# A hybrid decoder step, attention stage: VectorE's sample steps in other places, the last values loaded ahead of the gate tensor, GpSimd's products between the last six units

## The reference, cut to what matters

```python
p_c = _masked_probs(s_c, mask_c)
o_c = jnp.einsum('bqgrn,bngd->bqgrd', p_c.astype(v_cmp.dtype), v_cmp)
...
p_s = _masked_probs(s_s, mask_s[:, :, :, None, :])
o_s = jnp.einsum('bqgrk,bgqkd->bqgrd', p_s.astype(vg.dtype), vg)
...
p_w = _masked_probs(s_w, mask_w)
o_w = jnp.einsum('bqgrk,bkgd->bqgrd', p_w.astype(v_win.dtype), v_win)
return gates[..., 0:1] * o_c + gates[..., 1:2] * o_s + gates[..., 2:3] * o_w
...
br_b = jnp.einsum('btc,cd->btd', jax.nn.silu(zb) * yb, w_out_b)
```

## Time and profile before

| what | value |
|---|---|
| time, median of 3 runs | 2439.54 us (2439.12 to 2439.92) |
| profiled execution | 2440.18 us, of which span 2438.4 us |
| TensorE matmul busy | 2358.7 us (97%) |
| VectorE busy | 1228.0 us (50%) |
| ScalarE busy | 987.5 us (40%) |
| GpSimd busy | 208.4 us (9%) |
| mean granted TensorE clock | 0.993 |
| attention stage, units | about 810 to 1054 us in layer 0, 2019 to 2261 us in layer 1 |

### The profile page before, as it was taken

The page is one execution under the profiler, slowest core; times in us unless marked ns, Lnnn a source line. Parts: engine busy times, 40 slices in busy tenths (PEclk is TensorE's granted clock), DMA queues, the critical chain, the costliest instruction groups (busy, mean ns, idle before and its releaser), DMA issues.

```text
span 2438.4 us, 45717 instructions
## 1 busy us (share of the span) xinstructions
PE 2358.7 (97%) x18047; PEld 2065.0 (85%) x18047; DVE 1228.0 (50%) x2324; ACT 987.5 (40%) x2024; POOL 208.4 (9%) x349
## 2 busy tenths in 40 slices
PE   8999999999999999899989999999999999998998
PEld 8999999997788655589989999999977885555998
DVE  4444232546675566564454432224567656665544
ACT  4232223435564455532333221234446545554332
POOL 0000000000000233310000000000000002334000
PEclk9999999999999999999999999999999999999999
DMA  6343354707642677663234334547086318867530
GB/s 236 121 138 104 87 169 124 162 19 159 90 50 35 107 121 121 124 197 112 85 127 137 123 104 96 169 115 162 5 172 88 52 19 135 120 111 163 165 115 37
DMA packets 293309, 279.10 MB, mean 114 GB/s; under 512 B 92601, under 2 KB 281465, under 8 KB 291816
## 3 DMA queue, kind: packets, MB, share of 16 engines
q1 hardware_dynamic: 288680, 239.34, 44.9%
q0 software_dynamic: 4416, 36.85, 4.1%
HBM read 249.25 MB, written 43.53 MB: 120 GB/s over the span
## 4 chain that ended last, share of the span: by engine, by line
PE 88%; DVE 5%; ACT 3%; DMA 1%; issue 1%; SPq 1%; DVEq 0%; POOL 0%; ACTq 0%
PE ps L771 47%; PE ps L1016 13%; PE ps L942 7%; PE ps L1143 3%; PE ps L1167 3%; PE ps L1126 2%; PE ps L969 2%; DVE chL L2127 2%; PE ps L1265 2%; PE ps L1041 1%; ACT chH L1646 1%; DMA v_win<-in_state_win 1%; PE ps L1413 1%; SPq L569 1%; PE ps L1273 1%
## 5 line engine op out<-in xcount | busy, mean ns | idle before, releaser
L771 PE MATMUL ps<-hH,wH 128*128 128x272 f32 x2016 | 418.7, 289 | 8.4 <-DVE hL L1970 8.3
L771 PE MATMUL ps<-hH,wL 128*128 128x272 f32 x2016 | 420.4, 290 | 0.0
L405 DVE TENSOR_TENSOR wL<-w_raw,wH 128x2048 fp32r<-128x2048 f32 (+1 forms) x107 | 246.1, 2300 | 346.2 <-ACT wH L396 343.9
L771 PE MATMUL ps<-hL,wH 128*128 128x272 f32 x2016 | 417.4, 289 | 0.0
L771 PEld LDWEIGHTS ps<-hH,wH 128*128 128x128 f32 x2016 | 318.7, 189 | 10.2 <-issue 7.5
L771 PEld LDWEIGHTS ps<-hH,wL 128*128 128x128 f32 x2016 | 317.4, 189 | 0.0
L771 PEld LDWEIGHTS ps<-hL,wH 128*128 128x128 f32 x2016 | 317.4, 189 | 0.0
L2127 DVE TENSOR_TENSOR chL<-ps,chH 64x256 fp32r<-64x256 f32 x512 | 216.5, 423 | 158.9 <-ACT chH L1646 151.3
L1646 ACT ACTIVATE chH<-ps 64x256 fp32r<-64x256 f32 x512 | 206.8, 404 | 214.5 <-PE ps L1016 205.9
L396 ACT ACTIVATE wH<-w_raw 128x2048 fp32r<-128x2048 f32 (+1 forms) x107 | 204.8, 1914 | 97.3 <-PE ps L771 77.6
L741 POOL TENSOR_SCALAR pr<-pr,inv,zg 128x512 f32<-128x512 f32 (+3 forms) x256 | 153.0, 607 | 966.1 <-DVE inv L2317 966.1
(11 more groups left out here) (337 smaller groups left out, 4037.9 us busy)
## 6 DMA issues: line engine op xcount, KB each, us to landing
w_raw<-in_w_in SPq DMA_DIRECT2D x59, 1024.0 KB
craw<-in_cache_kv SPq DMA_DIRECT2D x256, 128.0 KB, 5.1
w_raw<-in_w_in SPq DMA_DIRECT2D x64, 256.0 KB
k_sel<-in_cache_kv SPq DMA_DIRECT2D x128, 128.0 KB, 5.5
v_sel<-in_cache_kv SPq DMA_DIRECT2D x128, 128.0 KB, 10.5
out_new_win_sample<-in_state_win POOLq DMA_DIRECT2D x16, 1016.0 KB, 6.1
w_raw<-in_w_out_a SPq DMA_DIRECT2D x8, 1024.0 KB
k_win<-in_state_win SPq DMA_DIRECT2D x16, 512.0 KB, 6.9
```

The costliest lines, as they stand in the source:

```text
L405: dve.tensor_tensor(block_part(wL, b), block_part(w_raw, b), block_part(wH, b).bitcast(F32), ALU.subtract).then_inc(w_lo, 1)
L771: last = nc.tensor.matmul(ps[:, bank + hf, 0:HALF], st, x[:, k, hf * HALF:(hf + 1) * HALF], start=k == 0 and w is wH and x is xH, stop=k = ...
```

## The change

Three engines' orders change; no operation is added or taken away.

SyncE: the load of `zbs` stands behind the values of pair 3, where it stood ahead of them. GpSimd: the seven products of `zbs` stood ahead of the scaling of unit 58; now two stand behind it and one behind each of units 59 to 63. VectorE: the gains of the back pair are computed behind the maxima at k = 2 (was k = 3), the first multiplication into `sy` joins the other two behind the maxima at k = 4 (was k = 3), and at k = 6 the inverses and the turned copy of the next and this unit are done ahead of `copy_turned` (were behind it, at k = 7).

```diff
--- before.py
+++ after.py
@@ -632,10 +632,10 @@
                         sp.wait_ge(s_fin, 4 * l + pair - 1)
                         load_half(l, pair - 1, numbers, 3, v_sel, v_win, s_v)
                     numbers, ahead = ahead, page_numbers(pair + 1) if pair < 3 else None
+                sp.wait_ge(s_fin, 4 * l + 3)
+                load_half(l, 3, numbers, 3, v_sel, v_win, s_v)
                 sp.wait_ge(sa_kt, 48 * l + 48)
                 sp.dma_start(zbs[:], a["zb_keep"][l].rearrange("k p t -> p k t")).then_inc(zb_back, 16)
-                sp.wait_ge(s_fin, 4 * l + 3)
-                load_half(l, 3, numbers, 3, v_sel, v_win, s_v)
 
                 def load_ob(i):
 
@@ -729,11 +729,6 @@
 
                 for i in range(UNITS):
                     n, at_u = P * (unit(i)[2] + 1), UNITS * l + i
-                    if i == 58:
-                        pool.wait_ge(zb_back, 16 * l + 16)
-                        pool.wait_ge(pa_o, 8 * l + 7)
-                        for c in range(KT - 1):
-                            pool.tensor_tensor(zbs[:, c, 0:SEQ], zbs[:, c, 0:SEQ], yT[:, c, 0:SEQ], ALU.mult).then_inc(a_p, 1)
                     gp, r, u, br = unit(i)
                     pool.wait_ge(pa_inv, at_u + 1)
                     for g in range(2):
@@ -741,6 +736,11 @@
                         last = pool.tensor_scalar(pr[i % 3][:, g, 0:n], pr[i % 3][:, g, 0:n], inv[:, i % 3, g:g + 1], zg[:, u, gate:gate + 1],
                                                   ALU.mult, ALU.mult)
                     last.then_inc(pa_sc, 1)
+                    if i == 58:
+                        pool.wait_ge(zb_back, 16 * l + 16)
+                        pool.wait_ge(pa_o, 8 * l + 7)
+                    for c in {58: (0, 1), 59: (2,), 60: (3,), 61: (4,), 62: (5,), 63: (6,)}.get(i, ()):
+                        pool.tensor_tensor(zbs[:, c, 0:SEQ], zbs[:, c, 0:SEQ], yT[:, c, 0:SEQ], ALU.mult).then_inc(a_p, 1)
 
                 pool.wait_ge(m_f, 8 * l + 8)
                 pool.dma_start(pin[:, 0:NT, :], a["p_prompt"][ds(l, 1)].rearrange("l b (t p) d -> p (l b t) d", p=P)).then_inc(p_in, 16)
@@ -2380,7 +2380,7 @@
                     last.then_inc(sa_drop, 1)
                     dve.drain()
 
-                def combine_first(pair, bank):
+                def combine_gains(pair):
 
                     c = 92 + 2 * (pair % 2)
                     dve.wait_ge(s_fin, 4 * l + pair + 1)
@@ -2389,12 +2389,12 @@
                     dve.reciprocal(small[:, 77:79], small[:, 96:98])
                     dve.drain()
                     dve.tensor_tensor(small[:, 80:83], grow[:, pair, :], small[:, 76:79], ALU.mult)
+
+                def combine(pair, bank):
+
+                    dve.wait_ge(sa_yt, 4 * l + pair)
                     dve.drain()
-                    dve.wait_ge(sa_yt, 4 * l + pair)
                     dve.tensor_scalar(sy[:], ps[:, bank, 0:P], small[:, 80:81], None, ALU.mult)
-
-                def combine_rest(bank):
-
                     for n in (1, 2):
                         dve.drain()
                         last = dve.scalar_tensor_tensor(out=sy[:], in0=ps[:, bank, n * P:(n + 1) * P], scalar=small[:, 80 + n:81 + n], in1=sy[:],
@@ -2466,7 +2466,7 @@
                 for i in range(UNITS):
                     mm, k = divmod(i, 8)
                     back, front = sample_block(mm)
-                    if i:
+                    if i and (k < 7 or back is None):
                         inverses(i)
                         turned(i - 1)
                     if k == 1 and (back, front) != (None, None):
@@ -2475,10 +2475,10 @@
                         maxima(i + 2)
                     if k == 3 and front is not None:
                         sample_bias(front, 1, swsc)
-                    if k == 3 and back is not None:
-                        combine_first(back, 6 + (mm + 1) % 2)
+                    if k == 2 and back is not None:
+                        combine_gains(back)
                     if k == 4 and back is not None:
-                        combine_rest(6 + (mm + 1) % 2)
+                        combine(back, 6 + (mm + 1) % 2)
                     if i == 1:
                         sample_gates()
                     elif i == 3:
@@ -2486,6 +2486,8 @@
                     elif i == 5:
                         sample_probs()
                     if k == 6 and back is not None:
+                        inverses(i + 1)
+                        turned(i)
                         copy_turned(mm)
                     if i == 62:
                         dve.wait_ge(zb_back, 16 * l + 16)
```

## The result

The changed kernel takes **2451.75 us** (median of 4 runs, 2449.72 to 2454.08) where the kernel before took 2439.33 us beside it (2436.01 to 2439.92): 12.4 us slower, a ratio of 1.0054 with a 95% interval of 1.0037 to 1.0071. The direction is the forecast one, the size is not: 2446.0 us were forecast, with a range up to 2451.0. The profiled execution took 2449.72 us, its span of 2447.9 us is 9.5 us longer than before, and all that follows accounts for these 9.5.

The account below looks back on a forecast made before the run. TensorE was taken as busy almost throughout, gains possible only where it waits. Per layer 0.6 + 2.5 + 0.5 - 0.4 = 3.2 us, twice 6.4, took 2439.54 to 2446.0 us; range 2440.5 to 2451.

Parts of the forecast that it names:

- What bounds the stage: Attention stage's end: the 4.6 us values wait goes; the weight block then holds `output(57)`, with TensorE idle some 6 us.
- Rival 1: Weight block not held, landing well earlier: `output(57)` 6.2 us sooner, 3.7 us per layer gained, 2432 us; chance 0.15.
- Part 1: Values loaded ahead of `zbs`: values land near 1022.1, weight block shifts +0.6 us per layer, bounds 0 and 1.1.
- Part 2: GpSimd's seven products among units 58 to 63 delay `output(63)`: +2.5 us per layer, bounds 0 and 8.6.
- GpSimd busy without a gap: Expected profile sign: GpSimd has no idle gap from unit 58 to the seventh product; gaps there would refute the prediction.
- Part 3: TensorE's half clock moves onto units 57 to 60, mostly hidden: +0.5 us per layer, bounds 0 and 1.0.
- keeps its distance: What follows `output(63)` (`put_out`, the split of `zbs`, the first tile) was to follow it at the same distance as before.
- Part 4: VectorE's moves in blocks 2, 4, 6, 7: 0.2 us each in blocks 2 and 4, -0.4 us per layer.
- nothing more: Behind unit 6 of a block, inverses ahead of `copy_turned` leave VectorE's total up to the next maxima unchanged: no further gain.
- The rule that was set aside: VectorE two-SBUF-input operations and GpSimd SBUF reads exclude each other; only the sample-column product would meet it, changing neither sum nor chances.
- the forecast's 0.54: Chance given to the forecast case, 2442.5 to 2451 us; the part above 2444.4 was to count as slower.

Follow-up runs that it names:

- weights first: Changed kernel with the first block of `w_out_b` issued between the last values and the gate tensor `zbs`: 2440.65 us.
- copy first: Changed kernel with `a_high(0)` and `a_low(0)` placed behind the turned copy of unit 63: 2446.30 us.
- gate in two: Changed kernel, unit 63 turned before `a_high(0)`, `a_low(0)`; `zbs` chunks 0-2 before values, 3-7 after weight block; products 0-2 before scaling 58, one behind each of 59-62: 2433.67 us.

## Why the prediction was right about the side and wrong about the size

**What bounds the stage: right.** The wait of L1235 for a transfer is gone in both layers, the values landed near 1021, 8.5 us behind their last issue at 1012.45 (forecast 1022.1), the weight block decides, TensorE idles 6.7 us ahead of `output(57)` (some 6 forecast), and `output(57)` stands at T + 6.15 (6.2). Rival 1, that the weights are not held, did not come about; the kernel with the weights first, where the block is early, gains 11 us, of the 14 that rival 1 and the forecast lie apart.

**Part 1 (the weight block's shift, +0.6 us per layer): not told from the forecast.** In the pair of profiled executions T - v0 grew by 0.1 and 2.2 us. Over the traces with the old order (three kernels, six values) it is 30.9 to 35.5, mean 32.9; with the new one (six kernels, twelve values) 33.4 to 34.9, mean 34.3. That is +1.4, above my upper bound of 1.1, but the six values of the old order scatter so much that the difference is uncertain by more than 1 us either way (an estimate from their spread). Why the old order scatters by more than 4 us and the new one by 1.5 is open.

**Part 2 (GpSimd's products, +2.5 us per layer): the chain was right, its end was not.** Step by step behind T, forecast and measured in layer 0: scaling 59 at 9.3 and 9.63, scaling 63 at 18.68 to 19.56 and 19.24, end of the seventh product at 20.80 and 21.62, ScalarE's copy at 21.45 and 22.21, `output(63)` at 21.9 and 23.54. Of the missing 1.6 us, 0.8 are GpSimd's own chain, drawn out by the turns it takes with VectorE: twice it waits 0.37 us for inverses whose clamp was held by its own products (units 59 and 61), and its scaling of unit 63 is 0.27 longer. "GpSimd busy without a gap", which the prediction had made a sign of being right, was wrong by these two waits. The other 0.8 are a step I left out: "turned copy of unit 63 at 21.45, `output(63)` 0.44 us later" took over the distance from the copy to `output(63)` from before. But there are two copies, one half each. Once ScalarE's `a_high(0)` is late, VectorE's `a_low(0)`, which stood out of the way before, is late as well, and it stands ahead of VectorE's half. I followed ScalarE's queue past the late product and not VectorE's.

**Part 3 (the clock, +0.5 us per layer): mis-sized, and at another place.** The low stretch behind `output(57)` was mostly hidden, as argued. The cost came at the end: TensorE, thinly used while GpSimd paces, and then waiting 2.65 us for the copy, ran `output(63)` at half clock, 1.97 us for 1.08, in both layers. That what follows `output(63)` "keeps its distance" failed by these 0.9 us. The kernel with the copy first shortens that wait to 0.48 us and has `output(63)` at full clock in both layers; it gains 5.5 us by the medians, where the trace of the changed kernel shows 2 x (0.8 + 0.9) = 3.4 for the two causes, and 2.2 between its own trace and that of the changed kernel behind T. The difference is not assigned. The low stretch behind `output(57)` is not hidden everywhere: with the copy first (layer 0), and with the gate in two, it was longer and held the chain up.

**Part 4 (VectorE, -0.4 us per layer): no gain measured alone** (0.9991 to 1.0009), and the argument had a gap. Ahead of the values the moves gain more than forecast: the first value transfer of layer 0 stands at 1000.19 to 1000.50 in the three kernels without them and at 997.87 to 999.70 in the eleven with them. But "nothing more" at unit 6 of a block was wrong in block 7, and part 2, which was to count that block, has no such term: VectorE's product on the sample columns, which `a_high(0)` waits for, stands behind `copy_turned`, and so behind the inverses and the turned copy that were moved ahead of it. In the kernel before it began at T + 16.20:

```profile
1050.09 0.42 DVE L2493 TENSOR_TENSOR zbs<-zbs,yT 128x256 f32<-128x256 f32 x1
```

With VectorE's part alone (T is 1033.62) it begins at T + 17.67:

```profile
1051.29 0.43 DVE L2495 TENSOR_TENSOR zbs<-zbs,yT 128x256 f32<-128x256 f32 x1
...
1051.81 0.66 ACT L1821 ACTIVATE bH<-zbs 128x544 fp32r<-128x544 f32 x1 [1.33 <-DVE zbs L2495]
...
1053.69 1.08 PE L1167 MATMUL ps<-prT,zv 128*64 128x512 f32 x4 [1.60 <-DVE prT L2323]
```

So `a_high(0)` and `a_low(0)` are late and in the way of unit 63's copies without any product of GpSimd's: `output(63)` waits 1.60 us for 0.48 and stands at T + 20.07 and 19.88 for 19.34 and 19.23. In that pair of traces, layers 0 and 1, the moves gain 2.05 and 1.75 us ahead of the values, lose 1.8 and nothing up to T, and lose 0.7 and 1.5 to the first tile: together nothing. The 1.8 us up to T may be the scatter of the old order; that is open.

**The rule that was set aside.** The prediction had from the Trainium skill ("SBUF — State Buffer", Who interferes with whom) that a VectorE operation with two SBUF inputs and a GpSimd one that reads SBUF exclude each other, and wrote that no row shows such a pair and that "it changes neither sum nor chances". The second half was wrong. By the rows, `make_low`, `a_low`, the product on the sample columns and the gain product all were lengthened beside GpSimd's products: 3.02 for 2.29, 1.35 for 0.73, 1.99 for 0.42 (weights first), 0.91 for 0.16. The trace agrees with the rule, also for the clamp of two numbers per partition (1.31 for 0.16), which has one SBUF input and is covered only if it ran in the page's two-port mode; the reciprocal, as small, took 0.17 us at most in every trace. Of these only the product on the sample columns had been named in the prediction. I had looked for the pair at one place and not gone through what the new order puts side by side.

**The sum.** Forecast per layer 0.6 + 2.5 + 0.5 - 0.4 = 3.2 us; measured in the profiled pair, mean of both layers, 1.2 ahead of T, 5.1 behind it, -1.5 ahead of the values: 4.8. The step that failed is the way from T to the first tile, 5.1 us for the 3.0 of parts 2 and 3. The forecast left out `a_low(0)` ahead of VectorE's copy of unit 63 (0.8 us), the lengthening of GpSimd's chain beside VectorE (0.8) and the half clock of `output(63)` (0.9), and had 0.5 for the clock at another place. So the profiled pair lies 3.2 us further apart than forecast. The other 2.8 of the 6.0 us between 12.4 and 6.4 belong to no step: the median of the changed kernel lies 2.0 us above its profiled execution, the fastest of the four, and that of the kernel before 0.85 below its own. In the chances, the forecast's 0.54 was counted as slower whole, though its range begins at 2442.5 and not at 2444.4.

## What to carry to other kernels

When a stall is removed, follow the transfer behind it in the queue: here the values' 4.6 us gave way to 6.7 us for the weight block, and only putting that block ahead of the gate made the swap pay. When a step becomes late, walk down the queue of every engine that feeds its consumer, not of one: whatever stood ahead of the other half "for free" is now in the way. Two different moves did that to the same copy here, GpSimd's and VectorE's. Work moved between GpSimd and VectorE has to be laid beside the other's two-input operations, down to the smallest; moving it off TensorE's path can put it onto theirs.

## What was not expected of the hardware

- Two operations on 128 x 2 and 128 x 3 numbers took 1.31 and 0.91 us for 0.16 beside GpSimd's two-input products, a reciprocal of 128 x 2 stayed at 0.17. The product on the sample columns (128 x 256) took up to 1.99 us for 0.42.
- Which side pays differs: seven products beside one `make_low` took 10.66 us for 8.61, three beside three `a_low` left the products at 3.71 (1.24 each) and drew the `a_low` out to 4.15 for some 2.2.
- TensorE fell to half clock a second time after a stretch in which it had been 3.02 of 5 us busy at full clock and a wait of 2.65 us. In the kernel before it was at full clock throughout a stretch with 8.69 of 10.22 us busy. With VectorE's part alone the wait ahead of `output(63)` was 1.60 us in both layers, and the work took 1.08 us in layer 0 and 1.90 in layer 1: the length of the wait alone does not tell. Why the two differ is open.
- The landing of the weight block, counted from the first value transfer, scattered between 30.9 and 35.5 us with `zbs` ahead of the values, and between 33.4 and 34.9 behind them.
